# The last expert's first four up slots loaded straight into the ring, the final norm's weights fetched last

## The chip, the cores and the metric

The kernel runs on one core of a Trainium2 chip. Its engines work side by side and meet at semaphores: TensorE (PE in the rows) multiplies, VectorE (DVE) and ScalarE (ACT) work on vectors, GpSimd (POOL) copies and issues transfers, and SyncE (SP) only issues transfers. The transfers of all of them (queue q1 for SP's, q0 for POOL's) share the core's 16 DMA engines. The metric is the time of the program in microseconds of device time, the median of several runs.

## What is computed

One decoder layer on 288 tokens (256 of a prompt, 32 of samples) of width 1024. Token mixing comes first; then every token goes through 4 of 32 experts, chosen by a router, and a final norm ends the layer. All is in float32. The part that matters here:

```
def expert_block(args):                 # 32 experts; a block is a group of rows of one expert
    xb, e = args
    gu = xb @ w_up[e] + b_up[e]         # w_up[e]: 1024 x 2048, 8 MB
    gate, up = gu[:, :D_EXPERT], gu[:, D_EXPERT:]
    gate = jnp.minimum(gate, 7.0); up = jnp.clip(up, -7.0, 7.0)
    act = (up + 1.0) * (gate * jax.nn.sigmoid(1.702 * gate))
    return act @ w_down[e] + b_down[e]  # w_down[e]: 1024 x 1024, 4 MB
...
x = x + moe(rmsnorm(x, norm_ffn_g), ...)
y_prompt = rmsnorm(xp, norm_final_g)    # y_sample likewise
```

## The kernel before

**Slots.** An expert's 12 MB of weights are cut into 12 slots of 1 MB (128 partitions x 2048 numbers): slots 0 to 7 hold `w_up`, 8 to 11 hold `w_down`. TensorE reads them from `ring`, which has room for exactly one expert. Behind it, `arena` holds nine parked slots (`parked[0]` to `parked[8]`, `PARKED = 9`): the next expert's slots 0 to 8 are fetched there by SP (`load_parked`, L409) while the ring is in use, and POOL copies them into the ring (`copy_slot`, L526 and L528, half a slot each) once TensorE has used the slot that lies there. Slots 9, 10 and 11 (`DIRECT`) are loaded by POOL straight from memory into the ring (`load_slot`, L532), also once TensorE has used the old ones.

**Items.** The work of an expert is cut into items of up to 32 rows. An expert has one item or more; its weights stay in the ring for all of them. TensorE's loop runs over 51 bodies; body i holds the up products of item i+1 (L1392, one group of 8 matmuls a slot, in the order k = 0 to 7) and the down products of item i (L1405, 16 matmuls a slot). They are interleaved: `up(0)` to `up(3)`, then the transposes of `turn_weights` (L1105), then `down(0)`, `up(4)`, `down(1)`, `up(5)`, `down(2)`, `up(6)`, `down(3)`, `up(7)`. After the last body, a tail does the activation and the four downs of the last item, the last sums (`combine`, L1170 and L1179), and the final norm.

**What sets the order.** The experts are processed in an order computed in the kernel (`order`); "place 30" is the last but one, "place 31" the last. For each place, POOL goes through `TURNS` = 0 to 7, 9, 8, 10, 11, and in each turn waits for TensorE's use of the slot by the last item of the place before (`up_used` or `down_used`). SP goes through slots 0 to 8 for the place after that, and waits before each until POOL's copy out of the parked slot is done (`slot_full`). So both are queues in a fixed order: a wait of one turn holds all that come behind it.

**The final norm's weights.** `fing` (128 x 1024, a broadcast) and `fingq` (128 x 256, in four pieces) are fetched on ScalarE's queue just before the expert loop (L689 and L692), `fing` into a part of `arena` behind the parked slots. VectorE uses them at L1088, in the last microseconds.

Of the kernel before, what the change touches and what calls it, by code (L numbers as in the profile page):

```python
# [26 lines left out]
P = 128  # L27
D = 1024
# [3 lines left out]
NS = DB * DS  # L32
# [8 lines left out]
NE = 32  # L41
TOPK = 4
BLK = NE
QN = P // BLK
MAX_ROUNDS = -(-T // BLK)
MAX_ITEMS = NE + (T * TOPK) // BLK
# [5 lines left out]
SLOT = 2048  # L52
UP_SLOTS = 8
DOWN_SLOTS = SLOTS - UP_SLOTS
PARKED = 9
BEHIND = 3
STAGED = [0, 1, 2, 3, 4, 5, 6, 7, 8]
DIRECT = [9, 10, 11]
TURNS = [0, 1, 2, 3, 4, 5, 6, 7, 9, 8, 10, 11]
EARLY_SLOTS = 5  # L60
ARENA = PARKED * SLOT + D
MIX_BLOCKS = 36
FILLS = MIX_BLOCKS // SLOTS
# [29 lines left out]
def hybrid_layer(nc, a, out):  # L93

    with ExitStack() as ctx:
        def sb(name, shape, dt=F32):
            return ctx.enter_context(nc.sbuf_tensor(name, shape, dt))

        def sem(name):
            return ctx.enter_context(nc.semaphore(name))  # L100
# [23 lines left out]
        items_before = sb("items_before", [1, NE], I32)  # L124
        order = sb("order", [1, NE], I32)
        stageq = sb("stageq", [P, 256])
        fingq = sb("fingq", [P, 256])

        arena = sb("arena", [P, ARENA])
        taken = [0]  # L130

        def region(n):
            lo = taken[0]
            taken[0] = lo + n
            assert taken[0] <= ARENA
            return arena[:, lo:lo + n]

        parked = [arena[:, k * SLOT:(k + 1) * SLOT] for k in range(PARKED)]
# [11 lines left out]
        rep4 = region(DB * DS)[0:DS].rearrange("p (b t) -> p b t", b=DB)  # L150
        region(EARLY_SLOTS * SLOT - taken[0])
        R1, R2, R4, R3 = (region(KC * T) for _ in range(4))
        fing = arena[:, PARKED * SLOT:PARKED * SLOT + D]

        def view(t, c):
            return t[:, :].rearrange("p (c t) -> p c t", c=c)
# [24 lines left out]
        def carve(region, n, rows=P):  # L181
            lo = pos[region]
            pos[region] = lo + n
            assert pos[region] <= regs[region].shape[1]
            return regs[region][0:rows, lo:lo + n]
# [19 lines left out]
        key_col, rank, place, blocks = (carve("prod", 1, NE) for _ in range(4))  # L205
# [17 lines left out]
        slot_full = [sem(f"slot_full{k}") for k in range(SLOTS)]  # L223
# [6 lines left out]
        bdown_in, fing_in = sem("bdown_in"), sem("fing_in")  # L230
        stored, v_stored, st_stored = sem("stored"), sem("v_stored"), sem("st_stored")
        old_rows_stored = sem("old_rows_stored")
        half_copied, slot_free = sem("half_copied"), sem("slot_free")
        up_used, down_used = sem("up_used"), sem("down_used")

        const_step, const_ready = sem("const_step"), sem("const_ready")
# [125 lines left out]
        def _(sp):  # L362
# [44 lines left out]
            def load_parked(e, k):  # L407

                sp.dma_start(parked[k], weights(e, k)).then_inc(parked_full[k], 16)  # L409

            def load_parked_again(place, after, ks):

                for k in ks:
                    sp.wait_ge(slot_full[k], place * 16 + 16 * FILLS)
                    load_parked(after, k)

            sp.wait_ge(sp_evac, 2 * G)
            sp.wait_ge(v_stored, 16)
            for k in range(EARLY_SLOTS):
                load_parked(1, k)  # L420
            for k in range(UP_SLOTS):
                sp.wait_ge(*mix_block_used(MIX_BLOCKS - SLOTS + k))
                load_slot(0, k)
                if k == 3:
                    load_parked(1, EARLY_SLOTS)
            sp.wait_ge(ya_evac, 2 * KC)
            for k in range(EARLY_SLOTS + 1, PARKED - 1):
                load_parked(1, k)
# [2 lines left out]
            load_parked(1, PARKED - 1)  # L431
            sp.wait_ge(before_known, 1)

            with sp.Fori(1, NE - 1) as place:
                after = sp.value_load(order[0:1, bass.ds(place + 1, 1)], min_val=0, max_val=NE - 1)
                load_parked_again(place + 1, after, STAGED)
            for tt in range(NT):
                sp.wait_ge(y_ready, tt + 1)
                if tt < 2:
                    sp.dma_start(out["y_prompt"][0, tt * P:(tt + 1) * P, :], xt[:, tt, :]).then_inc(stored, 16)  # L440
                else:
                    for q in range(QN):
                        sp.dma_start(out["y_sample"].rearrange("b t d -> (b t) d")[:, q * 256:(q + 1) * 256],
                                     xq[q * NS:(q + 1) * NS, :]).then_inc(stored, 16)
# [7 lines left out]
        def _(pool):  # L452
# [61 lines left out]
            def wait_used(before, k, turn):  # L514

                if k < UP_SLOTS:
                    pool.wait_ge(up_used, before * UP_SLOTS + (k + 1))
                else:
                    pool.wait_ge(down_used, before * DOWN_SLOTS + (k - UP_SLOTS + 1))
                pool.sem_inc(slot_free, 1)  # L520
                pool.wait_ge(slot_free, turn + 1)

            def copy_slot(e, k, n):

                pool.wait_ge(parked_full[k], 16 * e)
                nc.gpsimd.tensor_copy(ring[:, k, 0:D], parked[k][:, 0:D]).then_inc(half_copied, 1)  # L526
                pool.wait_ge(half_copied, (e - 1) * PARKED + n + 1)
                nc.gpsimd.tensor_copy(ring[:, k, D:SLOT], parked[k][:, D:SLOT]).then_inc(slot_full[k], 16)  # L528

            def load_slot(e, k):  # L530

                pool.dma_start(ring[:, k, :], weights(e, k)).then_inc(direct_full[DIRECT.index(k)], 16)  # L532
# [5 lines left out]
            for e in range(1, NE):  # L538
                before = pool.value_load(items_before[0:1, e - 1:e], min_val=0, max_val=MAX_ITEMS)
                here = pool.value_load(order[0:1, e:e + 1], min_val=0, max_val=NE - 1)  # L540
                for n, k in enumerate(TURNS):
                    wait_used(before, k, (e - 1) * SLOTS + n)
                    if k in STAGED:
                        copy_slot(e, k, STAGED.index(k))
                    else:
                        load_slot(here, k)

# [2 lines left out]
        def _(act):  # L550
# [117 lines left out]
            def take_rows(i):  # L668

                act.wait_ge(gathered, i + 1)  # L670
                nc.scalar.copy(xg, XB[:, 0:256]).then_inc(rows_ready, 1)
# [6 lines left out]
            def finish(i):  # L678
# [7 lines left out]
                nc.scalar.copy(out_sb, DN[:, 0:256]).then_inc(out_ready, 1)  # L686

            take_rows(0)
            act.dma_start(fing, a["norm_final_g"].rearrange("(l d) -> l d", l=1).to_broadcast([P, D])  # L689
                          ).then_inc(fing_in, 16)  # L690
            for q in range(QN):
                act.dma_start(fingq[q * NS:(q + 1) * NS, :],  # L692
                              a["norm_final_g"][q * 256:(q + 1) * 256].rearrange("(l d) -> l d", l=1).to_broadcast([NS, 256])
                              ).then_inc(fing_in, 16)
            act.wait_ge(gT_ready, 1)
            nc.scalar.copy(combT, TB[:, 0:T]).then_inc(combT_ready, 1)
            act.wait_ge(bdown_in, 16 * QN)
# [816 lines left out]
```

## Time and profile before

| | us |
|---|---|
| median of 3 runs | 1277.09 (1276.79 to 1278.07) |
| the profiled execution, its time | 1276.55 |
| its span in the trace | 1274.8 |
| mean granted TensorE clock | 0.984 of full speed |
| TensorE busy | 1155.6 (91% of the span) |
| POOL busy | 650.7 (51%) |
| moved by DMA | 449.06 MB, 352 GB/s over the span |

The profiled execution lies 0.5 us below the median of the runs, and its span 1.75 us below its own time. Times in the rows are counted from the start of the span. A line of a timeline gives the start, the duration, the engine, the line of the kernel, the operation and how many instructions are merged in it; in brackets stands how long the engine stood idle before it and what ended that. A busy TensorE is not one at its peak, since its matmuls are pipelined.

### The profile page before, as it was taken

What the parts mean: (1) busy time and instruction counts of PE and PEld (TensorE: products, weight loads), DVE (VectorE), ACT (ScalarE), POOL (GpSimd) and SP (SyncE); (2) the same over time, 40 slices, a digit from 0 to 9 for tenths busy, and PEclk for the clock granted to TensorE, in tenths of its full rate; (3) what the DMA queues carried; (4) which work ended last, traced back from release to release, by engine and by line L of the source; (5) the groups of instructions that cost most, each with busy time, mean ns of one, the idle gap of its engine ahead of it and who ended that gap; (6) DMA issues with size and microseconds to landing.
All of it is one profiled execution on the core that took longest, in us unless ns stands there. A gap on an engine that the chain in (4) does not pass through costs nothing.

```text
span 1274.8 us, 30490 instructions
## 1 busy us (share of the span) xinstructions
PE 1155.6 (91%) x11113; PEld 578.5 (45%) x11114; DVE 540.6 (42%) x1161; ACT 242.6 (19%) x483; POOL 650.7 (51%) x743
## 2 busy tenths in 40 slices
PE   8999999999999889888898998998988889889886
PEld 7877777775434333333233433333333333333232
DVE  1999984122633233433332343332333233323424
ACT  2012124000222122122122221221212111222122
POOL 0022300000566766857862678577576765756863
PEclk9999999999999999999999999998999999999998
DMA  9983433642899999999998999999999999999993
GB/s 261 341 272 109 135 131 135 264 168 101 354 422 402 422 421 422 422 422 421 422 422 374 367 407 422 422 422 422 422 415 422 422 422 422 421 422 422 422 421 153
DMA packets 94581, 449.06 MB, mean 352 GB/s; under 512 B 8526, under 2 KB 42894, under 8 KB 45339
## 3 DMA queue, kind: packets, MB, share of 16 engines
q1 hardware_dynamic: 79918, 345.88, 68.1%
q0 software_dynamic: 13872, 101.52, 19.3%
q10 hardware_dynamic: 749, 1.19, 0.3%
q8 instruction: 15, 0.25, 0.1%
q14 instruction: 27, 0.22, 0.0%
HBM read 447.00 MB, written 2.42 MB: 353 GB/s over the span
## 4 chain that ended last, share of the span: by engine, by line
PE 41%; DMA 27%; DVE 13%; POOL 8%; issue 8%; POOLq 1%; ACT 1%; DVEq 0%; SPq 0%; ACTq 0%
DMA ring<-in_w_down 19%; PE banks L1392 13%; DVE arena L815 8%; DMA arena<-in_w_up 8%; PE banks L1405 8%; PE banks L1190 8%; POOL ring L526 7%; PE banks L1105 3%; PE banks L1306 2%; PE banks L1170 2%; PE banks L1142 2%; PE banks L1179 1%; PE banks L1149 1%; POOL ring L528 1%; DVE arena L824 1%
## 5 line engine op out<-in xcount | busy, mean ns | idle before, releaser
L1392 PE MATMUL banks<-ring,hT 128*32 128x512 f32 x3328 | 419.2, 603 | 44.6 <-POOL ring L528 32.9
L526 POOL COPY ring<-arena 128x1024 f32<-128x1024 f32 x279 | 291.2, 1044 | 129.8 <-POOLq L520 127.4
L528 POOL COPY ring<-arena 128x1024 f32<-128x1024 f32 x279 | 292.6, 1049 | 36.9 <-POOL ring L526 0.9
L1405 PE MATMUL banks<-ring,hT 128*32 128x256 f32 x3328 | 224.4, 389 | 45.2 <-DMA ring<-in_w_down 44.9
L345 DVE TENSOR_TENSOR xq<-xq,banks 128x256 f32<-128x256 f32 x53 | 22.3, 421 | 500.7 <-PE banks L1179 500.7
L1392 PEld LDWEIGHTS banks<-ring,hT 128*32 128x32 f32 x3328 | 98.2, 110 | 203.6 <-issue 96.4
L1190 PE MATMUL banks<-hT,ring 128*128 128x288 f32 x768 | 190.5, 409 | 0.0
L1405 PEld LDWEIGHTS banks<-ring,hT 128*32 128x32 f32 x3328 | 101.3, 111 | 185.8 <-issue 78.6
L532 POOL DMA_DIRECT2D ring<-in_w_down x96 | 50.8, 529 | 257.3 <-POOLq L520 142.6
L1190 PEld LDWEIGHTS banks<-hT,ring 128*128 128x128 f32 x768 | 146.4, 192 | 40.2
L783 DVE TENSOR_SCALAR WT<-slot_ids,prod 128x128 f32 x153 | 86.6, 622 | 62.3 <-PE banks L1105 62.0
L815 DVE SCALAR_TENSOR_TENSOR arena<-arena 128x256 f32<-128x256 f32 x240 | 108.0, 523 | 0.0
L686 ACT COPY WT<-banks 128x256 f32<-128x256 f32 x52 | 19.4, 373 | 362.1 <-PE banks L1405 362.1
L773 DVE TENSOR_SCALAR WT<-slot_ids,prod,ss 128x32 f32 x104 | 67.3, 692 | 3.0
L1142 PE MATMUL banks<-xt,WT 128*32 128x256 f32 x832 | 59.3, 405 | 9.8 <-issue 8.8
L702 ACT ACT_TABLE_LOAD x51 | 65.4, 1283 | 1.5 <-issue 0.6
L1190 PE MATMUL banks<-arena,ring 128*128 128x288 f32 x256 | 62.3, 406 | 0.0
L1170 PE MATMUL banks<-WT 32*128 32x256 f32 x848 | 60.7, 400 | 0.7 <-issue 0.5
L681 ACT ACTIVATE hT<-hT 128x256 f32<-128x256 f32 x52 | 21.7, 417 | 184.8 <-DVE hT L1048 184.8
L1142 PEld LDWEIGHTS banks<-xt,WT 128*32 128x32 f32 x832 | 24.5, 115 | 67.8 <-issue 58.6
L1190 PEld LDWEIGHTS banks<-arena,ring 128*128 128x128 f32 x256 | 48.6, 190 | 13.4
L684 ACT COPY WT<-banks 128x288 f32<-128x288 f32 x52 | 20.8, 400 | 165.7 <-PE banks L1105 165.7
(250 smaller groups left out, 817.1 us busy)
## 6 DMA issues: line engine op xcount, KB each, us to landing
arena<-in_w_up SPq DMA_DIRECT2D x248, 1024.0 KB, 14.1
ring<-in_w_down POOLq DMA_DIRECT2D x96, 1024.0 KB, 11.4
arena<-in_w_down SPq DMA_DIRECT2D x31, 1024.0 KB, 16.2
ring<-in_w_in SPq DMA_DIRECT2D x24, 1024.0 KB, 10.2
ring<-in_w_up SPq DMA_DIRECT2D x8, 1024.0 KB, 4.8
ring<-in_w_branch_b SPq DMA_DIRECT2D x4, 1024.0 KB, 4.9
ring<-in_w_branch_a SPq DMA_DIRECT2D x4, 1024.0 KB, 4.8
ring<-in_w_out SPq DMA_DIRECT2D x4, 1024.0 KB, 4.9
```

The costliest lines, as they stand in the source:

```text
L526: nc.gpsimd.tensor_copy(ring[:, k, 0:D], parked[k][:, 0:D]).then_inc(half_copied, 1)
L528: nc.gpsimd.tensor_copy(ring[:, k, D:SLOT], parked[k][:, D:SLOT]).then_inc(slot_full[k], 16)
L532: pool.dma_start(ring[:, k, :], weights(e, k)).then_inc(direct_full[DIRECT.index(k)], 16)
L702: nc.scalar.activation(ss[:, 15:16], eps_col[:], ACT.Sigmoid)
L773: V.tensor_scalar(sel[:, tt, :], slot_ids[:, bass.ds(rank0, BLK)], rankm[:, tt, bass.ds(expert, 1)], ss[:, 4 + tt:5 + tt], ALU.is_equal, A ...
L783: ins = V.tensor_scalar(comb[:, tt], slot_ids[:, bass.ds(rank0, BLK)].unsqueeze(1).to_broadcast([P, QN, BLK]), rankm[:, tt, bass.ds(expert ...
L815: ins = V.scalar_tensor_tensor(acc, cprompt[:, c, k:k + SEQ], convw[:, c, k:k + 1], acc, ALU.mult, ALU.add)
L1142: mm(XB[q * BLK:(q + 1) * BLK, 0:256], sel[:, tt, :], xt[:, tt, q * 256:(q + 1) * 256], start=tt == 0, stop=False)
L1170: ins = mm(rows[:, q, :], combT[q * BLK:(q + 1) * BLK, tt * P:(tt + 1) * P], out_sb[q * BLK:(q + 1) * BLK, :], start=start, stop=stop)
L1190: ins = mm(dst[:, 0:T], w[:, k, h * P:(h + 1) * P], src[:, k, :], start=k == 0, stop=k == KC - 1)
L1392: ins = mm(UP[g * BLK:(g + 1) * BLK, :], xT[:, k, :], ring[:, k, g * 512:(g + 1) * 512], start=k == 0, stop=k == UP_SLOTS - 1)
L1405: ins = mm(DN[q * BLK:(q + 1) * BLK, 0:256], actT[:, f % 4, f // 4, :], ring[:, UP_SLOTS + j, h * D + q * 256:h * D + (q + 1) * 256], star ...
```

## The change

It touches the last place (31) and the norm's weights alone. SP's loop stops one place earlier, and the last place is written out behind it: SP fetches slots 4 to 7 to their parked places as before; then slots 0 to 3 straight into the ring, each behind a wait for TensorE's use of that slot in the last item of place 30 (`up_used`); then slot 8 to its parked place; then `fing` and `fingq`, now into `parked[2]` and `parked[3]`, which are free by then. POOL's last expert goes through `FINAL_TURNS`, without the turns 0 to 3. The five fetches of the norm's weights on ScalarE's queue go.

```diff
--- before.py
+++ after.py
@@ -57,6 +57,7 @@
 STAGED = [0, 1, 2, 3, 4, 5, 6, 7, 8]
 DIRECT = [9, 10, 11]
 TURNS = [0, 1, 2, 3, 4, 5, 6, 7, 9, 8, 10, 11]
+FINAL_TURNS = [4, 5, 6, 7, 9, 8, 10, 11]
 EARLY_SLOTS = 5
 ARENA = PARKED * SLOT + D
 MIX_BLOCKS = 36
@@ -124,7 +125,6 @@
         items_before = sb("items_before", [1, NE], I32)
         order = sb("order", [1, NE], I32)
         stageq = sb("stageq", [P, 256])
-        fingq = sb("fingq", [P, 256])
 
         arena = sb("arena", [P, ARENA])
         taken = [0]
@@ -150,7 +150,7 @@
         rep4 = region(DB * DS)[0:DS].rearrange("p (b t) -> p b t", b=DB)
         region(EARLY_SLOTS * SLOT - taken[0])
         R1, R2, R4, R3 = (region(KC * T) for _ in range(4))
-        fing = arena[:, PARKED * SLOT:PARKED * SLOT + D]
+        fing, fingq = parked[2][:, 0:D], parked[3][:, 0:256]
 
         def view(t, c):
             return t[:, :].rearrange("p (c t) -> p c t", c=c)
@@ -230,7 +230,7 @@
         bdown_in, fing_in = sem("bdown_in"), sem("fing_in")
         stored, v_stored, st_stored = sem("stored"), sem("v_stored"), sem("st_stored")
         old_rows_stored = sem("old_rows_stored")
-        half_copied, slot_free = sem("half_copied"), sem("slot_free")
+        half_copied, slot_free, final_free = sem("half_copied"), sem("slot_free"), sem("final_free")
         up_used, down_used = sem("up_used"), sem("down_used")
 
         const_step, const_ready = sem("const_step"), sem("const_ready")
@@ -431,9 +431,25 @@
             load_parked(1, PARKED - 1)
             sp.wait_ge(before_known, 1)
 
-            with sp.Fori(1, NE - 1) as place:
+            with sp.Fori(1, NE - 2) as place:
                 after = sp.value_load(order[0:1, bass.ds(place + 1, 1)], min_val=0, max_val=NE - 1)
                 load_parked_again(place + 1, after, STAGED)
+            final = sp.value_load(order[0:1, NE - 1:NE], min_val=0, max_val=NE - 1)
+            before = sp.value_load(items_before[0:1, NE - 2:NE - 1], min_val=0, max_val=MAX_ITEMS)
+            load_parked_again(NE - 1, final, range(UP_SLOTS // 2, UP_SLOTS))
+            for k in range(UP_SLOTS // 2):
+                sp.wait_ge(up_used, before * UP_SLOTS + (k + 1))
+                sp.sem_inc(final_free, 1)
+                sp.wait_ge(final_free, k + 1)
+                load_slot(final, k)
+            load_parked_again(NE - 1, final, range(UP_SLOTS, PARKED))
+            for k in range(2, 4):
+                sp.wait_ge(slot_full[k], (NE - 1) * 16 + 16 * FILLS)
+            load(fing, a["norm_final_g"].rearrange("(l d) -> l d", l=1).to_broadcast([P, D]), fing_in)
+            for q in range(QN):
+                load(fingq[q * NS:(q + 1) * NS, :],
+                     a["norm_final_g"][q * 256:(q + 1) * 256].rearrange("(l d) -> l d", l=1).to_broadcast([NS, 256]),
+                     fing_in)
             for tt in range(NT):
                 sp.wait_ge(y_ready, tt + 1)
                 if tt < 2:
@@ -520,11 +536,11 @@
                 pool.sem_inc(slot_free, 1)
                 pool.wait_ge(slot_free, turn + 1)
 
-            def copy_slot(e, k, n):
+            def copy_slot(e, k, copy):
 
                 pool.wait_ge(parked_full[k], 16 * e)
                 nc.gpsimd.tensor_copy(ring[:, k, 0:D], parked[k][:, 0:D]).then_inc(half_copied, 1)
-                pool.wait_ge(half_copied, (e - 1) * PARKED + n + 1)
+                pool.wait_ge(half_copied, copy + 1)
                 nc.gpsimd.tensor_copy(ring[:, k, D:SLOT], parked[k][:, D:SLOT]).then_inc(slot_full[k], 16)
 
             def load_slot(e, k):
@@ -538,10 +554,11 @@
             for e in range(1, NE):
                 before = pool.value_load(items_before[0:1, e - 1:e], min_val=0, max_val=MAX_ITEMS)
                 here = pool.value_load(order[0:1, e:e + 1], min_val=0, max_val=NE - 1)
-                for n, k in enumerate(TURNS):
+                turns = TURNS if e < NE - 1 else FINAL_TURNS
+                for n, k in enumerate(turns):
                     wait_used(before, k, (e - 1) * SLOTS + n)
                     if k in STAGED:
-                        copy_slot(e, k, STAGED.index(k))
+                        copy_slot(e, k, (e - 1) * PARKED + sum(k2 in STAGED for k2 in turns[:n]))
                     else:
                         load_slot(here, k)
 
@@ -686,12 +703,6 @@
                 nc.scalar.copy(out_sb, DN[:, 0:256]).then_inc(out_ready, 1)
 
             take_rows(0)
-            act.dma_start(fing, a["norm_final_g"].rearrange("(l d) -> l d", l=1).to_broadcast([P, D])
-                          ).then_inc(fing_in, 16)
-            for q in range(QN):
-                act.dma_start(fingq[q * NS:(q + 1) * NS, :],
-                              a["norm_final_g"][q * 256:(q + 1) * 256].rearrange("(l d) -> l d", l=1).to_broadcast([NS, 256])
-                              ).then_inc(fing_in, 16)
             act.wait_ge(gT_ready, 1)
             nc.scalar.copy(combT, TB[:, 0:T]).then_inc(combT_ready, 1)
             act.wait_ge(bdown_in, 16 * QN)
```

SP's queue, its end, before. L409 fetches to a parked slot, L405 to the ring; rows 40 to 59 are the loop over places, whose first rows (slots 0 to 3) are left out here:

```order
48 L409 ISA [waits slot_full4]
49 L409 DMA arena<-in_w_up 128x2048
...
54 L409 ISA [waits slot_full7]
55 L409 DMA arena<-in_w_up 128x2048
56 L409 ISA [waits slot_full8]
57 L409 DMA arena<-in_w_down 128x2048
58 L434 REGISTER_ALU
59 L434 COMPARE_AND_BRANCH
60 L440 DMA out_y_prompt<-xt 128x1024 [waits y_ready] x2
```

And after, the part written out for place 31, behind the same loop:

```order
64 L409 ISA [waits slot_full4]
65 L409 DMA arena<-in_w_up 128x2048
...
70 L409 ISA [waits slot_full7]
71 L409 DMA arena<-in_w_up 128x2048
72 L441 ISA
73 L405 REGISTER_ALU [waits up_used,final_free]
74 L405 DMA ring<-in_w_up 128x2048
...
82 L405 ISA [waits up_used,final_free]
83 L405 DMA ring<-in_w_up 128x2048
84 L409 ISA [waits slot_full8]
85 L409 DMA arena<-in_w_down 128x2048
86 L364 DMA arena<-in_norm_final_g 128x1024 [waits slot_full3,slot_full2]
```

Slots 0 to 3 of the last place have moved behind slots 4 to 7 and now wait for TensorE's use of the ring, no longer for POOL's copy; slot 8 and the norm's weights follow.

POOL's queue at its last place, before (rows 1253 to 1275 are eight pairs of copies, of which the first, the fourth and the fifth stand here):

```order
1250 L540 TENSOR_LOAD order
1251 L540 ISA x2
1252 L517 ISA
1253 L526 COPY ring<-arena 128x1024 [waits up_used,parked_full0,slot_free]
1254 L528 COPY ring<-arena 128x1024 [waits half_copied]
...
1262 L526 COPY ring<-arena 128x1024 [waits up_used,parked_full3,slot_free]
1263 L528 COPY ring<-arena 128x1024 [waits half_copied]
1264 L517 REGISTER_ALU
1265 L526 COPY ring<-arena 128x1024 [waits up_used,parked_full4,slot_free]
```

And after:

```order
1250 L556 TENSOR_LOAD order
1251 L556 ISA x2
1252 L533 ISA
1253 L542 COPY ring<-arena 128x1024 [waits up_used,parked_full4,slot_free]
1254 L544 COPY ring<-arena 128x1024 [waits half_copied]
```

The four pairs for slots 0 to 3 are gone; the rest of the place follows in the order of before. TensorE's queue is the same in both: it still takes slot 0 first and slot 7 last.

## Rows read from the trace of the kernel before

**Rows 1.** Windows: busy us (x count) by engine, TensorE's granted clock, DMA share, GB/s.

```profile
1100.00:1160.00 60.00, 52.18 (x627) 21.02 (x623) 19.64 (x40) 11.78 (x23) 40.05 (x43) 1.00 1.01 422
...
1232.60:1243.60 11.00, 8.29 (x85) 2.78 (x77) 4.96 (x10) 1.84 (x5) 9.58 (x10) 1.00 1.01 422
1243.60:1248.10 4.50, 4.46 (x65) 1.88 (x65) 2.26 (x3) 0.40 (x1) 4.24 (x5) 1.00 0.10 42
```

**Rows 2.** Timeline of POOL at the last place: its first copy, its last, its direct loads.

```profile
1233.37 1.04 POOL L526 COPY ring<-arena 128x1024 f32<-128x1024 f32 x1 [0.84 <-POOLq L520]
...
1249.71 1.04 POOL L528 COPY ring<-arena 128x1024 f32<-128x1024 f32 x1
1250.69 0.53 POOL L532 DMA_DIRECT2D ring<-in_w_down  x1
...
1253.38 1.08 POOL L532 DMA_DIRECT2D ring<-in_w_down  x2
```

**Rows 3.** Timeline of TensorE in the last body and behind it.

```profile
1242.11 1.07 PE L1392 MATMUL banks<-ring,hT 128*32 128x512 f32 x8 [1.09 <-POOL ring L528]
...
1250.80 1.07 PE L1392 MATMUL banks<-ring,hT 128*32 128x512 f32 x8 [0.23 <-POOL ring L528]
...
1257.54 0.58 PE L1105 MATMUL banks<-ident,WT 128*128 128x128 f32 x3 [3.15 <-DVE hT L1057]
```

**Rows 4.** The same engine in the body before, whose ups and downs never wait.

```profile
1220.89 3.64 PE L1392 MATMUL banks<-ring,hT 128*32 128x512 f32 x32 [0.22 <-DVE hT L791]
...
1231.06 1.04 PE L1392 MATMUL banks<-ring,hT 128*32 128x512 f32 x8
```

**Rows 5.** Chain that ended last: last up load to tail's downs (start, us, what).

```profile
1220.19 27.96 DMA arena<-in_w_up
...
1258.12 5.28 PE banks L1405 x64
```

**Rows 6.** SP's issues of the last place's slots 4, 5, 6 (timeline), then landings.

```profile
1212.78 0.33 SPq L409 DMA_DIRECT2D arena<-in_w_up  x1
1214.94 0.33 SPq L409 DMA_DIRECT2D arena<-in_w_up  x1
1217.71 0.33 SPq L409 DMA_DIRECT2D arena<-in_w_up  x1
...
arena<-in_w_up SPq DMA_DIRECT2D x1, 1024.0 KB, 19.8
...
arena<-in_w_up SPq DMA_DIRECT2D x1, 1024.0 KB, 22.7
...
arena<-in_w_up SPq DMA_DIRECT2D x1, 1024.0 KB, 25.5
```

**Rows 7.** DMA issues, us to landing: POOL's at 1228.59 and 1232.01, SP's slot 8.

```profile
ring<-in_w_down POOLq DMA_DIRECT2D x1, 1024.0 KB, 9.5
...
ring<-in_w_down POOLq DMA_DIRECT2D x1, 1024.0 KB, 16.3
...
arena<-in_w_down SPq DMA_DIRECT2D x1, 1024.0 KB, 19.1
```

**Rows 8.** Windows around two waits of TensorE for a transfer: 1120.7 and 1210.2.

```profile
1120.70:1123.70 3.00, 0.04 (x4) 0.00 (x0) 0.00 (x0) 0.00 (x0) 2.87 (x4) 1.00 1.01 421
1123.80:1130.00 6.20, 6.03 (x78) 2.84 (x78) 0.76 (x2) 2.71 (x5) 5.41 (x6) 1.00 1.02 423
1210.20:1213.10 2.90, 0.00 (x0) 0.00 (x0) 0.00 (x0) 0.00 (x0) 2.77 (x4) 1.00 1.03 427
...
1214.30:1217.60 3.30, 3.30 (x28) 0.92 (x24) 0.00 (x0) 2.33 (x4) 2.55 (x3) 0.50 1.03 427
```

**Rows 9.** The norm's weights: issues with landing; chain near them; first use (timeline).

```profile
arena<-in_norm_final_g ACTq DMA_DIRECT2D x1, 512.0 KB, 7.4
...
355.79 15.18 DMA ring<-in_w_down
...
1267.67 1.28 DVE L1088 SCALAR_TENSOR_TENSOR xt<-xt,ss,arena 128x1024 f32<-128x1024 f32 x1
```

## Prediction

> **What bounds the kernel now.** I read the windows first. From 1100 to 1160 us the DMA share is 1.01 at 422 GB/s, while TensorE is busy 52 of 60 us: weights set the pace in the steady state [rows 1]. A slot of 1 MB (1.05 million bytes) at 422 GB/s takes 2.48 us of all 16 engines. The change acts on the last place, so I then read what ends last there. After 1243.6 the DMA share falls to 0.10, and TensorE's clock is full [rows 1]: memory is no longer the limit. POOL starts its first copy of place 31 at 1233.37 and starts the last half at 1249.71, done at 1250.75: eight slots in 17.4 us, 2.17 us each, with next to no gap [rows 2]. TensorE waits 1.09 us for a copy before `up(3)` at 1242.11, and `up(7)` starts at 1250.80, right behind the last copy [rows 3]. So the last body is paced by POOL. The chain names the transfer of slot 7, issued at 1220.19 and landed 27.96 us later, at 1248.15, as what came before the last copy [rows 5]; both were within half a microsecond of each other. This landing is the number that matters below.
>
> **What the change removes.** Four slots fewer to copy: 4 x 2.17 = 8.7 us of POOL. Started at 1233.4, its four copies would end at 1242.1 instead of 1250.75. If all else stood, `up(7)` could start some 8 us earlier. It does not stand, because two other orders decide then.
>
> **What it moves: SP's queue.** The eight up loads of place 31 keep their number but change their order: 4, 5, 6, 7, then 0, 1, 2, 3. Slots 4 to 7 are issued when they were, since the POOL copies of place 30 they wait for are not touched: the fifth and sixth issue of before, at 1212.78 and 1214.94, are now the first two places in the queue's work of slots 4 and 5 [rows 6]. Slots 0 to 3 wait for `up(0)` to `up(3)` of place 30's only item, which run from 1220.89 to 1224.53 [rows 4]; so they are issued between about 1222 and 1225, where in the kernel before four loads had gone out earlier. Does the queue run dry meanwhile? The fifth load of before landed at 1212.78 + 19.8 = 1232.6, the sixth at 1214.94 + 22.7 = 1237.6, the seventh at 1217.71 + 25.5 = 1243.2, the eighth at 1248.15 [rows 5, 6]. Counted back from the fifth in steps of 2.48 us, the first landed near 1222.7. So SP's queue had about 20 us of work ahead in the DMA engines, and what now enters it at 1212.78 to 1225 is still there before its turn comes. A load counts as landed when the last of 16 engines has its share; this slowest engine stays full, also if the others idle for half a microsecond. So the landing times stay and only their names change: slot 0 lands at 1232.6, slot 1 at 1237.6, slot 2 at 1243.2, **slot 3 at 1248.15**.
>
> The last three are 5.0 to 5.6 us apart, not 2.48, because POOL's direct loads of place 30, issued from 1228.59 and landed at 1238.1 to 1248.3, take every other turn of the same engines [rows 7]. These loads do not change: they hang on the downs of the body before.
>
> **What it meets: TensorE's order.** TensorE takes slot 0 first. `up(0)` at 1236.4 finds its slot, `up(1)` about so, `up(2)` waits until 1243.2 and `up(3)` until 1248.2. Behind `up(3)` in TensorE's queue stand `turn_weights`, four downs of place 30 and `up(4)` to `up(7)`, all of whose weights have lain ready since 1242. In the kernel before, this work ran during POOL's copies; now all of it comes behind the last landing. Its length is read from the body before, which never waits: from the end of its `up(3)`, 1220.89 + 3.64 = 1224.53, to the start of `up(7)`, 1231.06, are 6.5 us [rows 4]. With 1.07 us for `up(3)` itself, `up(7)` starts at 1248.2 + 1.1 + 6.5 = 1255.8 and not at 1250.8: **+5.0 us**.
>
> **The clock.** With 1.1 us for one up, `up(2)` waits some 4.4 us (1238.8 to 1243.2) and `up(3)` 3.9 us (1244.3 to 1248.2). The trace has two waits of about 3 us for a transfer: after the one at 1120.7 the granted clock stayed at 1.00, after the one at 1210.2 it fell to 0.50, the lower of the two levels (1.2 GHz), for 3.3 us [rows 8]. In the 7.6 us behind `up(3)` such a fall would cost half of 3.3 to 3.4 us, 1.7 us. Bounds: 0 and, if it lasts twice as long, 3.4. Two waits in a row, both longer than those of the trace, make me take **+1.7 us**.
>
> The Trainium skill (TensorE: Matmul & The Clock Gate, section HAM oscillation) describes this pattern, a wait for a transfer behind which the next burst starts at half rate each time. By that rule the 1.7 us are certain; the rows show it once and once not, so I take it for likely.
>
> **Behind the last up.** The same tail follows: `up(7)` at 1250.80, the transposes at 1257.54, four downs in 5.28 us [rows 3, 5]; it shifts as a whole. POOL's direct loads of place 31 wait for downs 1 to 3 of place 30; they were issued from 1250.69, and the pair from 1253.38 [rows 2]. There the second of the pair started within 1.1 us of 1253.38, and the fourth down ran without a wait to 1263.4 [rows 5]. Now the downs of place 30 that free the slots come with the burst, the last of them about 0.9 us before `up(7)`, so slot 11 goes out near 1256, some 2 us later than it did, while the downs of the tail come 5 us later: its cover grows by about 3 us. Upper bound: with SP's loads for company the first such load took 9.5 us [rows 7], which gives 1265.5, still before the last down's 1263.4 + 5.0 - 1.7 = 1266.7. So 0 on the path.
>
> **The norm's weights.** 0.66 MB leave the start of the expert loop: at 422 GB/s 1.6 us of DMA. At the end they go behind slot 8, which lands at 1231.5 + 19.1 = 1250.6 [rows 7], so they are in by about 1252.5, long before their first use at 1267.67 [rows 9], and ahead of slot 9's data. Cost 0; what hides it is the tail of 15 us. Five issues leave ScalarE's queue at a time when no one waits for it. Is the 1.6 us a gain? Only if the path from there to the end passes the DMA engines' total work. The chain's first transfer behind them starts at 355.79, after an unbroken run of TensorE, and takes 15.18 us [rows 9], three slots in alternation with SP's; that time hangs on SP's queue being filled, not on how far ahead it is. So I take 0, with bounds of -1.6 and 0.
>
> **Sum.** 1276.55 + 5.0 + 1.7 + 0 = 1283.25 for an execution like the profiled one; with the median 0.5 us above it, **1283.8 us**, about 0.5% slower.
>
> **The rivals.**
> *A, the ring loads are not slowed (faster).* If slots 1 to 3 landed 2.48 us apart, slot 3 would be in at 1240.1 and the burst would start 8 us earlier. For it: they are issued before POOL's direct loads. Against it: so were the loads of before, and they landed 5 us apart; and the bytes are the same, so POOL's slot 11 of place 30, needed by `down(3)`, would still land near 1248.3 [rows 7]. Then `down(3)` and `up(7)` follow: `up(7)` at about 1249.3, -1.5 us, and with the norm's 1.6 us -3.1: 1274.0.
> *B, the slowest engine catches up (no change).* From 1243.6 to 1248.1 only a tenth of the DMA engines' time is used [rows 1]. If the pause that slots 0 to 3 leave evened out the 16 engines, slot 3 would land at 1243.6 and `up(7)` start at 1251.2: +0.4, with or without part of the clock's 1.7 and the norm's 1.6: 1275.9 to 1279.2, middle 1277.5. It decides in this way once slot 3 lands before 1243.2 + 1.5. Against it: that engine has work all the time in both kernels.
> *C, the forecast's mechanism without the clock's fall.* +5.0 and up to -1.6: 1280.5 to 1282.1. It is part of the likeliest case, not of its opposite.
>
> **How the numbers follow.** The forecast with C: 0.78, of this about 0.5 with a clock fall (1282.2 to 1283.8, up to 1286 with a longer fall) and 0.28 without. B: 0.12. A: 0.10. A measurement of this kernel tells about 0.2%, 2.6 us, from no change; nearly all of the forecast's case lies above 1279.7, B within 1274.5 to 1279.7, A below or at its edge. So slower 0.78, same 0.13, faster 0.09. The case's own range is 1280 to 1286; with half of B it becomes 1277.0 to 1286.0, which leaves out A and the rest of B.
>
> **What would show it.** Right: four L526/L528 pairs at the last place, ended by about 1242; slot 3's load, issued near 1225, landing near 1248; two waits of TensorE of about 4 us for `ring<-in_w_up` at L1392, then an unbroken run of ups and downs of 7 to 9 us; the clock at 0.50 in it; a span near 1281.5. Wrong: slot 3 landing before 1244 (B, or A if the direct loads land later in exchange), or every stage from 400 us on earlier by 1.6 us (the norm's weights do count).

## The result and the profile after

The changed kernel takes 1285.34 us (median of 5 runs, 1283.67 to 1288.42), the kernel before 1277.09 us (1275.13 to 1278.07). The ratio is **1.0071, with a 95% interval of 1.0054 to 1.0089**: slower. By the medians that is +8.3 us, by the ratio +9.1 us; the forecast was +6.7, with a range of 1277.0 to 1286.0 us. The median lies within that range, the ratio's 1286.2 us (1.0071 times 1277.09) just above it. Two more comparisons, on other chips, gave 1.0061 (1.0041 to 1.0082) and 1.0059 (1.0040 to 1.0079). The profiled execution took 1285.21 us, its span 1283.5 us, 8.7 us more than before. Single runs of one kernel spread by several us (1273.9 to 1282.7 for the kernel before in the longest series), so no single run decides anything below. One run of the kernel before took 2276.83 us and is left out of the ratios.

Line numbers after differ from those before: the ups are L1403 (L1392), the downs L1416 (L1405), POOL's copies L542 and L544 (L526 and L528), its direct loads L548 (L532). First TensorE's timeline at the last place, from `up(0)` to `up(7)`, to be read against [rows 3, 4]:

```profile
1235.41 1.07 PE L1403 MATMUL banks<-ring,hT 128*32 128x512 f32 x8 [3.86 <-DMA ring<-in_w_up]
1241.03 1.93 PE L1403 MATMUL banks<-ring,hT 128*32 128x512 f32 x8 [4.55 <-DMA ring<-in_w_up]
1244.78 1.94 PE L1403 MATMUL banks<-ring,hT 128*32 128x512 f32 x8 [1.82 <-DMA ring<-in_w_up]
1247.52 1.94 PE L1403 MATMUL banks<-ring,hT 128*32 128x512 f32 x8 [0.81 <-DMA ring<-in_w_up]
...
1250.25 1.94 PE L1416 MATMUL banks<-ring,hT 128*32 128x256 f32 x16
1251.96 1.91 PE L1403 MATMUL banks<-ring,hT 128*32 128x512 f32 x8
...
1258.00 1.03 PE L1403 MATMUL banks<-ring,hT 128*32 128x512 f32 x8
```

Four ups that wait for transfers, then the burst: from here on that is the unbroken work from the start of `up(3)` to the start of `up(7)`. An up takes 1.93 us where it took 1.07; `up(0)`, behind the first wait, still took 1.07. The issues of slots 0 and 3 (timeline of SP) and their us to landing:

```profile
1219.70 0.34 SPq L405 DMA_DIRECT2D ring<-in_w_up  x1
...
1221.71 0.33 SPq L405 DMA_DIRECT2D ring<-in_w_up  x1
...
ring<-in_w_up SPq DMA_DIRECT2D x1, 1024.0 KB, 15.7
...
ring<-in_w_up SPq DMA_DIRECT2D x1, 1024.0 KB, 25.8
```

Slot 0 landed at 1235.4, slot 3 at 1247.5. POOL had long been done: its last copy of slots 4 to 7 ended at 1237.4, and then its queue stood still for 18 us, until `down(1)` of place 30 let it issue slot 9:

```profile
1236.32 1.04 POOL L544 COPY ring<-arena 128x1024 f32<-128x1024 f32 x1
1255.54 0.53 POOL L548 DMA_DIRECT2D ring<-in_w_down  x1 [18.18 <-POOLq L536]
...
1258.95 0.53 POOL L548 DMA_DIRECT2D ring<-in_w_down  x1 [0.20 <-issue]
```

The windows (busy us and count of PE, PEld, DVE, ACT, POOL; granted clock; DMA share; GB/s) show what no row of before did: the clock at half for 17 us on end. The first row is an earlier wait, for a `w_down` slot at 1208.4, as there is one in the kernel before at 1213.2. The last row is the tail: half the clock for 6.8 us.

```profile
1204.00:1214.00 10.00, 6.95 (x80) 2.59 (x76) 0.00 (x0) 2.70 (x5) 6.24 (x6) 0.83 0.98 383
1236.60:1253.60 17.00, 9.95 (x51) 2.25 (x55) 0.86 (x3) 0.40 (x1) 0.76 (x1) 0.50 0.50 205
1247.50:1258.00 10.50, 10.48 (x100) 3.80 (x104) 0.86 (x3) 0.40 (x1) 2.33 (x3) 0.70 0.14 33
1263.90:1270.70 6.80, 6.20 (x55) 3.03 (x59) 2.68 (x3) 0.40 (x1) 0.00 (x0) 0.50 0.17 72
```

In the kernel before the clock was at half in the tail too, for 3.3 us:

```profile
1258.70:1262.00 3.30, 3.30 (x36) 1.74 (x32) 0.95 (x1) 0.00 (x0) 0.00 (x0) 0.50 0.45 191
```

The chain of the changed kernel, against [rows 5]:

```profile
1221.71 25.77 DMA ring<-in_w_up
...
1247.52 1.94 PE banks L1403 x8
...
1265.40 6.25 PE banks L1416 x64
```

**The 8.7 us.** The last landing moved from 1248.15 (slot 7) to 1247.5 (slot 3): -0.7. From the start of `up(3)` to that of `up(7)` there are 10.5 us (1247.52 to 1258.00), where the body before the last needs 7.6: 2.9 are the clock's. `up(7)` so starts at 1258.00 and not at 1250.80, +7.2. Behind it the four downs of the tail take 6.25 us, not 5.28, and the rest of the tail some 0.5 more: +1.5, with the clock at half for twice as long there.

**That split is of one pair of executions.** Five executions with the direct loads ahead of this burst were profiled: the one above, two more of the changed kernel and two of the direct loads alone (both are told below). Against the one trace of before their spans are 7.1 to 10.8 us longer, 8.9 on the mean. In each the order makes 5.0 of it: from the last landing to `up(7)` it is 7.6 us at full clock, where it was 2.65. The clock in the burst makes 1.5 to 3.1, mean 2.5. The last landing, 1248.15 before, lay between 1247.4 and 1252.3, mean +1.3. The tail from `up(7)` on took 22.1 to 25.5 us, and 24.0 before: mean +0.2. `up(3)` in the execution with the latest landing:

```profile
1252.35 1.93 PE L1403 MATMUL banks<-ring,hT 128*32 128x512 f32 x8 [0.82 <-DMA ring<-in_w_up]
```

So nothing shows that the tail's +1.5 is the change's. The tail's four downs ran wholly at full clock in one execution of the direct loads alone (first row), and for the most part at half in the version below with the lowest ratio, in which slots 4 to 7 go direct and POOL is held (second row):

```profile
1266.77 3.66 PE L1416 MATMUL banks<-ring,hT 128*32 128x256 f32 x64
...
1255.78 6.03 PE L1418 MATMUL banks<-ring,hT 128*32 128x256 f32 x64
```

### The profile page after: what moved, and what is told of

Same layout as the page of the kernel before. It is cut to its first block, busy times and chain, and to the rows that moved or that the text cites. A ratio compares the mean times of both kernels' runs of the same rounds, so it can differ in the third digit from the quotient of the medians.

```text
span 1283.5 us, 30474 instructions
## 1 busy us (share of the span) xinstructions
PE 1157.4 (90%) x11113; PEld 578.8 (45%) x11114; DVE 538.9 (42%) x1161; ACT 242.4 (19%) x483; POOL 642.1 (50%) x735
## 4 chain that ended last, share of the span: by engine, by line
PE 44%; DMA 23%; DVE 13%; issue 9%; POOL 8%; POOLq 1%; ACT 1%; SPq 0%; DVEq 0%; ACTq 0%
DMA ring<-in_w_down 19%; PE banks L1403 14%; PE banks L1416 9%; DVE arena L826 8%; PE banks L1201 8%; POOL ring L542 7%; PE banks L1116 4%; PE banks L1317 2%; DMA arena<-in_w_up 2%; PE banks L1181 2%; PE banks L1153 2%; DMA ring<-in_w_up 2%; PE banks L1190 1%; PE banks L1160 1%; POOL ring L544 1%
## 5 line engine op out<-in xcount | busy, mean ns | idle before, releaser
L1403 PE MATMUL banks<-ring,hT 128*32 128x512 f32 x3328 | 421.8, 607 | 52.0 <-POOL ring L544 29.6
L542 POOL COPY ring<-arena 128x1024 f32<-128x1024 f32 x275 | 286.4, 1041 | 139.1 <-POOLq L536 127.8
L544 POOL COPY ring<-arena 128x1024 f32<-128x1024 f32 x275 | 287.9, 1047 | 36.3 <-POOL ring L542 0.9
L1416 PE MATMUL banks<-ring,hT 128*32 128x256 f32 x3328 | 225.0, 390 | 44.6 <-DMA ring<-in_w_down 44.3
L1403 PEld LDWEIGHTS banks<-ring,hT 128*32 128x32 f32 x3328 | 98.7, 110 | 211.5 <-issue 95.7
L1416 PEld LDWEIGHTS banks<-ring,hT 128*32 128x32 f32 x3328 | 101.5, 111 | 186.4 <-issue 81.4
L548 POOL DMA_DIRECT2D ring<-in_w_down x96 | 50.7, 529 | 263.4 <-POOLq L536 148.4
```

The lines of the kernel that those rows point to most:

```text
L1403: ins = mm(UP[g * BLK:(g + 1) * BLK, :], xT[:, k, :], ring[:, k, g * 512:(g + 1) * 512], start=k == 0, stop=k == UP_SLOTS - 1)
L1416: ins = mm(DN[q * BLK:(q + 1) * BLK, 0:256], actT[:, f % 4, f // 4, :], ring[:, UP_SLOTS + j, h * D + q * 256:h * D + (q + 1) * 256], star ...
```

## The experiments

Ratios are to the kernel before, run on the same chip beside the other. The edits are shortened; they start from the changed kernel, but that of the norm's weights alone starts from the kernel before.

**Which half of the change?** First the direct loads alone:

```diff
-            load(fing, ...); load(fingq[...], ...)       # SP, last
+            act.dma_start(fing, ...); act.dma_start(fingq[...], ...)   # ScalarE, ahead of the loop
-        fing, fingq = parked[2][:, 0:D], parked[3][:, 0:256]
+        fing = arena[:, PARKED * SLOT:PARKED * SLOT + D]; fingq = sb("fingq", [P, 256])
```

> The direct loads alone: slots 0 to 3 of the last place go straight into the ring as in the change, the norm's weights are fetched early on ScalarE's queue into their own buffers as before. My theory (all of the loss comes from slot 3 landing last with the rest of TensorE's body behind it; the norm's weights count for nothing): 1285 us, within 1.5 us of the changed kernel, 0.6% above before. Rival (the norm's late fetch is worth its 1.6 us of DMA): 1287 us, 1.6 above the changed kernel. Rival (the norm's late fetch costs, in company of the last slots): 1280 us or less.

Measured: 1283.44 us, 1.0047 (1.0034 to 1.0061). That is 1.9 us below the changed kernel, a little more than the 1.5 us that I had allowed. But the changed kernel had been timed on another chip, so the two were run together later:

> The changed kernel once more, as the common measure of the three that follow on this chip. 0.6 to 0.7% above before.

> The direct loads without the norm's late fetch, beside the changed kernel on the same chip, since the first comparison (0.47% against 0.71% above before) was made on two. My theory (the late fetch is free, the difference was how long the low clock lasted): within 0.2% of the changed kernel. Rival (the late fetch costs 2 us in company of the direct loads): 2 us and more below it.

Measured: the change 1285.33 us, 1.0059 (1.0040 to 1.0079); the direct loads alone 1285.29 us, 1.0072 (1.0050 to 1.0093). No difference can be seen. Then the norm's weights alone:

```diff
+            for k in range(2, 4):
+                sp.wait_ge(slot_full[k], NE * 16 + 16 * FILLS)    # place 31's copies are out
+            load(fing, ...); load(fingq[...], ...)                # SP, behind the last slot
```

> The norm's weights alone: all slots of the last place are parked and copied as before; SP fetches the norm's weights last, into parked places 2 and 3, once POOL has copied the last place's slots out of them. My theory: 1277.1 us, no difference beyond 0.1%. Rival (1.6 us of DMA work less ahead of the last place shows at the end): 1275.5 us. Rival (the late fetch lies on the path): 1279 us or more.

Measured: 1278.25 us, before 1278.13; 1.0004 (0.9989 to 1.0018). The interval goes from 1.4 us below to 2.3 us above. All of the loss is the direct loads'; the norm's late fetch is neither a gain nor a loss that can be measured.

**Is it the loads into the ring, or the order?** Three runs change only who comes behind whom. In the first, SP issues the ring loads ahead of the parked ones:

```diff
-            load_parked_again(NE - 1, final, range(UP_SLOTS // 2, UP_SLOTS))
             for k in range(UP_SLOTS // 2):
                 ...
-            load_parked_again(NE - 1, final, range(UP_SLOTS, PARKED))
+            load_parked_again(NE - 1, final, range(UP_SLOTS // 2, PARKED))
```

> The change with SP's order alone undone: slots 0 to 3 go straight into the ring as in the change, but ahead of the parked slots 4 to 7, so that the eight land in the order in which TensorE takes them. Slot 0 can only be issued when place 30's up(0) is done, and slots 4 to 7 wait behind it. My theory (the order of landing is the loss, not the loads into the ring): slot 7 lands last, at 1248 to 1251, is copied in 2.2 us and has one up behind it: 1278 to 1281 us, 4 to 6 us below the changed kernel; a gap of 1 to 3 us in the DMA engines' work near 1219 to 1224. Rival (loads into the ring are what costs): as the changed kernel.

Measured: 1279.44 us, 1.0005 (0.9989 to 1.0020); the changed kernel on the same chip:

> The changed kernel once more, as it is, beside the three that follow, since one trace cannot tell how long the low clock lasts from run to run. My theory: 0.5 to 0.8% above before, slot 3 landing at 1246 to 1251 in the trace, TensorE waiting some 3 to 5 us each for slots 1 and 2, the clock at 0.50 for 3 us or more of the burst behind slot 3. With the tail's clock full as in the run with the norm's weights early, 1283.5; with it low, 1285.5. Rival (the fetch of the norm's weights costs time at the end): 1285 or more and the same for all its runs.

gave 1286.69 us, 1.0061 (1.0041 to 1.0082). The order alone undone, the loss is gone, although slots 0 to 3 still go straight into the ring. Its windows and SP's issues of slots 0 and 7, with us to landing:

```profile
1216.00:1222.00 6.00, 5.78 (x61) 2.40 (x57) 4.97 (x10) 0.82 (x2) 5.10 (x6) 1.00 0.42 143
...
1218.69 0.34 SPq L405 DMA_DIRECT2D ring<-in_w_up  x1
...
1223.34 0.37 SPq L409 DMA_DIRECT2D arena<-in_w_up  x1
...
ring<-in_w_up SPq DMA_DIRECT2D x1, 1024.0 KB, 6.2
...
arena<-in_w_up SPq DMA_DIRECT2D x1, 1024.0 KB, 26.4
```

Of the up slots, slot 7 landed last, at 1249.7, with its copy and one up behind it. (What ended last there ran through slot 8, landed at 1253.2, and slot 11, for which the last down waited 1.1 us.) The expected gap of the DMA engines is there (share 0.42 for 6 us) and cost nothing: more on that below.

In the second, TensorE's order is made to follow the landings. The last body is written out behind the loop:

```diff
+            with pe.Fori(0, bodies - 1) as i:
+                one_body(i, range(UP_SLOTS))
+            one_body(bodies - 1, [4, 5, 6, 7, 0, 1, 2, 3])
```

> The changed kernel with TensorE's last body written out behind the loop and its ups in the order of the landings: 4, 5, 6, 7, 0, 1, 2, 3, the downs interleaved as before. Nothing else. My theory (the landings stay; what stood behind slot 3 in TensorE's order was the loss): one up behind slot 3's landing instead of up(3) to up(7) and four downs, 6.5 us and more gone: 1277 to 1279 us. POOL's first direct load of place 31 then goes out earlier and takes turns with slot 3's, as it did with slot 7's in the run with slots 4 to 7 direct, which costs 2.5 us of it. Rival (the last landing moves by as much as the order gains): above 1283.

Measured: 1279.35 us, 1.0012 (0.9996 to 1.0028). That is close to the 1277 to 1279 us expected. But its timeline has no wait for a ring load at all, only for POOL's copies, so here the time bears out the mechanism and not the trace: in this execution TensorE came to the last body 8.7 us later than in that of the changed kernel (ready at 1240.2, not 1231.5), and its last up, `up(3)`, started at 1253.63 right behind the one before. The turn-taking with POOL's load, which I expected, could not be seen in it.

In the third, the slots that go direct are the last four in TensorE's order:

```diff
-FINAL_TURNS = [4, 5, 6, 7, 9, 8, 10, 11]
+FINAL_TURNS = [0, 1, 2, 3, 9, 8, 10, 11]
-            load_parked_again(NE - 1, final, range(UP_SLOTS // 2, UP_SLOTS))
-            for k in range(UP_SLOTS // 2):
+            load_parked_again(NE - 1, final, range(UP_SLOTS // 2))
+            for n, k in enumerate(range(UP_SLOTS // 2, UP_SLOTS)):
```

> The change with one thing other: the four slots that go straight into the ring are 4 to 7 and not 0 to 3; slots 0 to 3 are parked and copied. SP's order is 0 to 3, then 4 to 7, and POOL copies 0 to 3. TensorE takes them in that order. My theory (the loss is that the last landing has seven of TensorE's groups behind it; now it has one up): up(7) starts 1.1 to 3.3 us earlier than before, as soon as slot 7 has landed: 1274 to 1276 us. Rival (loads into the ring are slow or late whatever their place in the order): near 1285 us.

Measured: 1278.40 us, 1.0005 (0.9989 to 1.0021). The loss is gone, the gain I expected on top (1 to 3 us) is not. Timelines of POOL, SP and TensorE, and landings:

```profile
1244.33 0.53 POOL L548 DMA_DIRECT2D ring<-in_w_down  x1 [5.23 <-POOLq L536]
...
1229.40 0.33 SPq L405 DMA_DIRECT2D ring<-in_w_up  x1
...
ring<-in_w_up SPq DMA_DIRECT2D x1, 1024.0 KB, 24.4
...
1253.84 1.89 PE L1403 MATMUL banks<-ring,hT 128*32 128x512 f32 x8 [2.23 <-DMA ring<-in_w_up]
```

Slot 7 landed at 1229.4 + 24.4 = 1253.8; slot 6, issued at 1227.68 with 21.2 us to landing, at 1248.9. They are 5 us apart, since POOL had issued slot 9 of place 31 at 1244.33 and its load took every other turn. (The profiled execution, 1282.40 us, was the slowest of the 12.) The earlier the downs run, the earlier POOL's loads come in ahead of the last up slot. So POOL was made to wait:

```diff
-FINAL_TURNS = [0, 1, 2, 3, 9, 8, 10, 11]
+FINAL_TURNS = [0, 1, 2, 3, 9, 10, 11, 8]
+                    if e == NE - 1 and k == DIRECT[0]:
+                        pool.wait_ge(slot_full[UP_SLOTS - 1], NE * 16 + 16 * FILLS)
```

> Slots 4 to 7 straight into the ring and 0 to 3 copied, and besides POOL holds its own direct loads of the last place until slot 7 has landed, and copies slot 8 behind them. In the run without this hold, slot 7 landed 5.0 us behind slot 6 because POOL's load of slot 9 took turns with it. My theory: slot 7 lands 2.5 us behind slot 6 and up(7) starts there: 2.5 us below that run, 1275.5 to 1276.5 us where before has 1277 to 1278, 0.1 to 0.2% below before. Rival (what is held then comes too late for the tail's downs): no better than before.

Measured: 1275.92 us (1272.14 to 1277.95, 12 runs), before 1277.02; 0.9992 (0.9979 to 1.0006). Slot 7 now landed 3.0 us behind slot 6 (1245.2 and 1248.2). Its chain and its timeline of TensorE at `up(7)`:

```profile
1227.40 20.76 DMA ring<-in_w_up
...
1255.85 5.96 PE banks L1418 x64
...
1248.21 1.07 PE L1405 MATMUL banks<-ring,hT 128*32 128x512 f32 x8 [1.05 <-DMA ring<-in_w_up]
```

`up(7)` starts at 1248.2, upon the landing, 2.6 us ahead of the kernel before; the span is only 1.2 us shorter, as the tail's clock was at half for longer. The median is 1.1 us below before and 2.5 below the version without the hold (other chip), but the interval includes no difference: the lowest ratio of all versions, and not shown to beat the kernel before.

**What does the clock cost?** TensorE was kept busy in the waits by matmuls of no use (their result goes to a free bank):

```diff
+                    for _ in range(busy.get(k, 0)):      # last body only, ahead of up(k)
+                        mm(XB[:, 0:256], ones[:], slot_ids[:, 0:256], start=True, stop=True)
```

> The changed kernel with the last of TensorE's bodies written out behind the loop, and matmuls of no use (7, 10 and 8 of 128x256, 0.43 us each at full clock, into a free bank) ahead of up(1), up(2) and up(3), so that TensorE is busy where it waits for slots 1, 2 and 3. The trace of the changed kernel shows the granted clock at 0.50 from 1236.6 for 17 us, and the burst behind slot 3 takes 10.5 us where the body before takes 7.6. My theory (that clock is due to the waits and costs 2.9 us in the burst): 1282.4 us, the clock at 1.00 in the burst, up(7) 7.6 us behind the start of up(3). Up to 1.5 us more if the tail's longer fall goes too: 1281. Rival (order alone, the clock costs nothing that the landings do not hide): 1285.3. Rival (the useless matmuls delay up(3) itself): 1286 or more.

Measured: 1289.08 us (1284.37 to 1294.31), 1.0105 (1.0087 to 1.0123): slower, in the direction of the third theory named there. The window of its burst and its timeline around `up(3)`:

```profile
1251.00:1258.60 7.60, 7.60 (x104) 3.38 (x107) 0.86 (x3) 0.40 (x1) 2.35 (x3) 1.00 0.16 41
...
1247.33 3.72 PE L1476 MATMUL banks<-slot_ids,ones 128*128 128x256 f32 x16
1250.98 1.06 PE L1403 MATMUL banks<-ring,hT 128*32 128x512 f32 x8
```

The clock stayed full and the burst took 7.6 us, as forecast; but the last eight useless matmuls (16 in the row) put `up(3)` 2.2 us behind slot 3's landing. That accounts for this execution alone, 1284.37 us, the fastest of the five; why the other four took 1288.8 to 1294.3 us no trace shows. With fewer of them:

> As the run with useless matmuls in the waits, but 6, 7 and 3 ahead of up(1), up(2) and up(3) (2.8, 3.3 and 1.4 us at full clock) where it had 7, 10 and 8, which lasted 3.3, 4.6 and 3.7 us and put up(3) 2.2 us behind the landing of slot 3. My theory (the low clock costs 2.9 us in the burst, the rest is the order): up(3) within 0.3 us of slot 3's landing, the clock at 1.00 in the burst, which takes 7.6 us; 2 to 4 us below the changed kernel of the same call, still 3 to 5 us above before. Rival (the clock costs nothing): as the changed kernel. If the clock is low all the same, the useless matmuls last twice as long and it is slower than the changed kernel by some 3 us.

Measured: 1286.06 us, 1.0054 (1.0035 to 1.0074), beside 1286.69 for the change. Again 7.6 us for the burst, but `up(3)` started 1.9 us late: the clock had already fallen in the wait for slot 0, which nothing covered, and the first six matmuls took 4.24 us instead of 2.8. The 2 to 4 us that I expected to gain did not come. The third try leaves none ahead of `up(3)`:

> As the run with useless matmuls in the waits, but 4, 7 and 4 ahead of up(0), up(1) and up(2) and none ahead of up(3) (1.7, 3.0 and 1.7 us at full clock; 0.43 us each), so that none of them stands between slot 3's landing and the burst, and the first wait, behind which the clock fell in the runs before, is covered in part. My theory (3 us of the burst are the clock's): up(3) within 1 us of slot 3's landing, a burst of 7.6 us, 2 to 3 us below the changed kernel. Rival (the clock costs only where the landings hide it): no difference.

Measured: 1282.60 us, 1.0047 (1.0030 to 1.0064), beside 1285.33 for the change, 1.0059 (1.0040 to 1.0079). The windows ahead of the burst and of it (with `up(2)`):

```profile
1235.40:1245.60 10.20, 6.01 (x18) 3.54 (x19) 0.85 (x2) 0.00 (x0) 1.72 (x2) 0.50 1.01 421
1249.10:1258.10 9.00, 9.00 (x110) 3.84 (x113) 0.86 (x3) 0.40 (x1) 2.32 (x3) 1.00 0.11 30
```

`up(3)` started some 1.4 us behind its landing, up to half a microsecond more than expected, and the clock was full from then on. By the medians 2.7 us were gained, of the 2 to 3 expected; the two intervals overlap, so the traces carry this better than the times. At full clock the burst took 7.6 us (the two runs above); in the four profiled executions with direct loads first and no useless matmuls, besides the one shown, it took 9.1, 9.5, 10.6 and 10.7 us. The clock's price there is 1.5 to 3.1 us in the traces, and it varies from run to run with how long the clock stays low. That the waits bring the clock down is borne out by the bursts: at full clock in all three runs whose waits were filled, in part at half in all five whose waits were not. What the clock costs in whole runs is not clear of noise.

## Why the prediction came out as it did

The sign, the mechanism and the size of its main term were right; the sum was too small. In the profiled pair it was short by 2.0 us: the clock took 1.2 more in the burst than its term and 1.5 more in the tail, and the landing came 0.7 earlier. Over the five executions it was short by 2.2: 0.8 the clock in the burst, 1.3 the landing, 0.2 the tail. So the clock's term was too small either way, and the landing, taken over unchanged, had no term for its spread.

- *What bounds the kernel, and what goes.* Right. POOL's queue was free 18 us before it was needed; nothing came of it.
- *SP's queue: the landings stay and change their names.* Right within a microsecond in this execution for the one that counts: slot 3 at 1247.5, forecast 1248.15. In part that was luck: in the other four with direct loads first it landed at 1247.4, 1249.9, 1250.2 and 1252.3. The forecast took its value from one execution and gave it no bounds. Slots 0 to 2 landed at 1235.4, 1241.0 and 1244.7, forecast 1232.6, 1237.6 and 1243.2. The steps differ because in this execution POOL's direct loads of place 30 came 4.7 us earlier and took their turns in other places; what the last of them costs is the same.
- *TensorE's order.* Right: forecast +5.0 for the order with the landing kept. Measured +7.2 for `up(7)`, less 2.9 for the clock, is 4.3, and with the 0.7 by which slot 3 was earlier it is 5.0. The three order experiments each bring the kernel back to 1.0005 to 1.0012 and leave the direct loads in place.
- *The clock.* **This is the step that failed, a term mis-sized.** Forecast +1.7 in the burst, bounds 0 and 3.4; measured 2.9 there, and 1.5 to 3.1 (mean 2.5) over the five executions. I priced one fall of the length of the nearest row (3.3 us, [rows 8]). But with four waits, and one up between each two, the clock stayed low from the second up on: it stood at 0.50 for 17 us, of which 6.1 lay in the burst. The first of the waits, for slot 0, I had excluded, because I took `up(0)` to be ready later (1236.4) than its slot (1232.6); here it was ready at 1231.5 and waited 3.9 us. The Trainium skill (TensorE: Matmul & The Clock Gate, section HAM oscillation) describes a loop whose work of about 2 us is shorter than each wait for a transfer, and which starts at the low clock behind every wait. This trace agrees with it for `up(1)` to `up(3)`, at 1.93 us each, and not for `up(0)`, at 1.07 us.
- *The tail.* The covers held: slot 11, issued at 1258.95, cost no wait, and the chain does not pass it. In this pair "it shifts as a whole" was wrong by 1.5 us, the clock again; on the mean of the five it holds within 0.2 us. The forecast had no term for how the tail's clock varies, -1.9 to +1.5 us, and nothing shows that the change moves it.
- *The norm's weights.* Right: 0, by two comparisons.
- *The rivals.* A did not come about: the up loads landed 5.6, 3.8 and 2.7 us apart, with POOL's among them. B did not: the last landing did not come early in any of the five. C, the case without the clock's fall, is ruled out for every profiled execution of the change.
- *The time against the median.* The stages ahead of the last place ended 4.7 us earlier in the profile after than in that before (TensorE's last wait for a `w_down` slot ended at 1208.4, not 1213.2). Yet its last landing came only 0.7 us earlier. What ties the two is open: in the five executions slot 3 landed 25.3 to 25.9 us behind its issue, and the later TensorE was ready for the last body (1231.3 to 1237.1), the later came issue and landing. In the execution in which TensorE was about as late as before (1237.1, before 1236.2) slot 3 landed at 1252.3, 4.2 us behind the forecast.

## What to carry to other kernels

A transfer that is moved later in a queue must be priced by what stands behind it in the consumer's order, not by the work it saves: here 8.7 us of POOL's copies went, and five ups and four downs that used to run during them came to stand behind the last landing. Let the last landing be the last thing that the consumer takes, and look at who takes turns on the same DMA engines just then. When one change lets an engine wait several times in close succession, price its clock for the whole stretch, not for one fall. And take a landing that the sum hangs on from more than one execution: here it moved by 5 us between runs of the same order.

## What the hardware showed that was not expected

**The last landing hardly moves with a gap in the transfers.** With the ring loads first, the DMA engines stood at a share of 0.42 for 6 us, yet slot 0 landed at 1224.9, slot 1 at 1227.4 (1219.55 and 7.8 us) and the last one at 1249.7, within the 1247.4 to 1252.3 us of the kernels with direct loads first and without the gap. A reading that fits is that of [rows 1]: a tenth of the engines' time was in use from 1243.6 to 1248.1 while the last up slot was still out. One engine of 16 lags, and a landing is its own. The landing events in the traces bear this out: of slot 7's 16 shares in the kernel before, fifteen were in by 1237.0 and the last at 1248.15; with the gap, fifteen by 1248.5 and the last at 1249.7. So the gap took the lead from the fifteen, and the last one came 1.5 us later than before. The lag grows while the engines are full: in the kernel before, the last share came less than 0.1 us behind the fifteenth for the up load issued at 702.79, just after a stretch with a DMA share of 0.76 (690 to 700 us), and 5.2 us behind it for that issued at 1206.25. Which engine lags, and why, was not looked into.

**A later issue may land first.** In the changed kernel SP issued the norm's weights at 1227.23, behind slot 8 at 1226.80; their landing took 17.9 us, to 1245.1, while slot 8's took 23.1, to 1249.9:

```profile
arena<-in_norm_final_g SPq DMA_DIRECT2D x1, 512.0 KB, 17.9
...
arena<-in_w_down SPq DMA_DIRECT2D x1, 1024.0 KB, 23.1
```

So the order of a queue is not the order of landings, at least not between a broadcast and a plain load.

**The low clock can last.** 17 us in the window shown above, and 20.4 us in another execution of the same kernel, against 3.3 us in [rows 8]:

```profile
1235.90:1256.30 20.40, 12.21 (x63) 2.65 (x67) 3.48 (x8) 0.40 (x1) 3.52 (x4) 0.50 0.56 232
```
